# Gathering expert rows on TensorE: one-hot selection for two experts at a time, two down buffers, and norms without GpSimd

## The reference, cut to what matters

```python
x = _ln_affine(ALPHA * x + gate1 * t, ln1_g, ln1_b)      # t: output projection of the mixer
h = (_layer_norm(x) * (1 + scale2) + shift2)             # "h2" in the kernel
f = _hier_moe(h)      # best of 4 groups, best 2 of its 8 experts, for each token
x = _ln_affine(ALPHA * x + gate2 * f, ln2_g, ln2_b)
# an expert: (silu(xb @ w_exp_gate[e]) * (xb @ w_exp_up[e])) @ w_exp_down[e]
```

## Time and profile before

| | us |
|---|---|
| median of 3 runs | 1001.75 (999.08 to 1003.87) |
| the profiled execution: its time | 1002.76 |
| its span, first to last instruction | 1001.2 |
| PE busy | 874.3 (87%) |
| DVE busy | 379.3 (38%) |
| ACT, POOL busy | 209.4, 141.8 |
| HBM read, written | 284.46 MB, 25.45 MB |

### The profile page before, as it was taken

One profiled execution on the slowest core, in us unless ns is written; L12 is line 12 of the kernel. 1 busy time (PEld: TensorE's weight loads), 2 busy tenths in 40 slices (PEclk: granted clock), 3 DMA queues, 4 the chain that ended last, 5 costly groups with the idle time before them and its releaser, 6 DMA issues.

```text
span 1001.2 us, 12712 instructions
## 1 busy us (share of the span) xinstructions
PE 874.3 (87%) x4001; PEld 502.7 (50%) x4002; DVE 379.3 (38%) x672; ACT 209.4 (21%) x302; POOL 141.8 (14%) x192
## 2 busy tenths in 40 slices
PE   3789999999999999969778888997868888887895
PEld 2457677888888887859323233332223233322231
DVE  4522443565343247896412222222122122212145
ACT  2321334441234244122300000000000000000024
POOL 2210267000001000340300000000000000000041
PEclk9799999999999999986999999999999999999998
DMA  9894653365647624449699999999999999999984
GB/s 366 325 299 172 218 206 138 115 236 187 236 181 192 206 86 149 146 158 426 224 419 424 426 426 428 427 426 427 427 428 427 427 427 425 431 425 429 422 337 133
DMA packets 52557, 310.50 MB, mean 310 GB/s; under 512 B 5058, under 2 KB 7202, under 8 KB 36898
## 3 DMA queue, kind: packets, MB, share of 16 engines
q1 hardware_dynamic: 41104, 272.64, 67.2%
q0 software_dynamic: 10800, 35.64, 10.4%
q10 hardware_dynamic: 610, 1.66, 0.6%
HBM read 284.46 MB, written 25.45 MB: 310 GB/s over the span
## 4 chain that ended last, share of the span: by engine, by line
PE 60%; DMA 22%; DVE 6%; issue 3%; SPq 3%; ACT 3%; POOL 1%; DVEq 0%; POOLq 0%; ACTq 0%
PE bank L684 58%; DMA up_w<-in_w_exp_up 18%; DMA modraw<-in_w_mod 2%; SPq L385 2%; PE bank L942 1%; DVE hid L1888 1%; ACT sg L1297 1%; DVE res L1661 1%; DMA y_first<-round_y,pos_y 1%; DMA packed_x<-h,pos 1%; ACT hid_t L1072 1%; PE bank L881 1%; PE bank L876 1%; POOL packed_x L608 1%; DMA round_y<-yout 0%
## 5 line engine op out<-in xcount | busy, mean ns | idle before, releaser
L684 PE MATMUL bank<-gate_w,x_t 128*64 128x512 f32 x512 | 234.2, 611 | 28.7 <-DMA up_w<-in_w_exp_up 20.6
L684 PE MATMUL bank<-up_w,x_t 128*64 128x512 f32 x512 | 234.3, 612 | 0.0
L684 PEld LDWEIGHTS bank<-gate_w,x_t 128*64 128x64 f32 x512 | 70.6, 141 | 183.4 <-issue 180.0
L684 PE MATMUL bank<-down_w,hid_t 128*64 128x512 f32 x496 | 121.7, 636 | 14.7 <-ACT hid_t L1072 14.7
L684 PE MATMUL bank<-h_hi,w_hi 128*128 128x512 f32 x320 | 126.5, 395 | 1.6 <-ACT h_hi L1106 1.6
L684 PE MATMUL bank<-h_hi,w_lo 128*128 128x512 f32 x320 | 126.3, 395 | 0.0
L684 PE MATMUL bank<-h_lo,w_hi 128*128 128x512 f32 x320 | 125.0, 398 | 0.0
L1888 DVE TENSOR_TENSOR hid<-bank,sg 64x512 f32<-64x512 f32 x31 | 21.5, 693 | 226.7 <-ACT sg L1297 226.7
L1437 DVE TENSOR_TENSOR w_lo<-raw,w_hi 128x1024 fp32r<-128x1024 f32 x56 | 68.6, 1227 | 78.6 <-ACT w_hi L1072 78.5
L1297 ACT ACTIVATE sg<-bank 64x512 f32<-64x512 f32 x31 | 18.3, 590 | 378.8 <-PE bank L684 378.8
L615 POOL DMA_DIRECT2D round_y<-yout x31 | 16.1, 519 | 423.3 <-issue 423.3
(11 more groups left out here) (328 smaller groups left out, 1005.8 us busy)
## 6 DMA issues: line engine op xcount, KB each, us to landing
down_w<-in_w_exp_down SPq DMA_DIRECT2D x32, 2048.0 KB, 30.3
gate_w<-in_w_exp_gate SPq DMA_DIRECT2D x31, 2048.0 KB, 24.9
up_w<-in_w_exp_up SPq DMA_DIRECT2D x31, 2048.0 KB, 29.6
modraw<-in_w_mod SPq DMA_DIRECT2D x24, 1024.0 KB, 8.4
raw<-in_w_in SPq DMA_DIRECT2D x9, 2048.0 KB, 9.7
round_y<-zrow POOLq DMA_DIRECT2D x6, 2048.0 KB, 7.6
xrows<-packed_x SPq DMA_DIRECT2D x32, 256.0 KB, 20.9
raw<-in_w_branch_b SPq DMA_DIRECT2D x2, 2048.0 KB, 9.4
```

Of the source, the lines that this page charges most:

```text
L684: return pe.matmul(out, lhsT, rhs, start=start, stop=stop, skip_group_check=True)
```

## The change

- The table `packed_x`, its scatter, and every load of rows go away. h2 is split into two fp32r parts, `h2_hi` (ACT) and `h2_lo` (DVE, h2 less h2_hi), once, behind expert 0. For a pair of experts DVE writes a one-hot matrix `sel` (128 tokens x 4 tiles x 2 experts x 64 slots, fp32r), and PE multiplies it with the two parts: eight matmuls (4 tiles x 2 parts) give 512 of the 1024 columns of both experts' rows. One half is formed in the even expert and the other in the odd one. ACT copies the result to SBUF (`x_rows`), PE transposes it (4), DVE copies it to `x_t`.
- `h2_hi` takes the place of the third down buffer. There are two for down and still three for gate and up; SP issues gate and up of e, then down of e-1, which waits for `down` of e-3.
- The loop goes over six experts (four times), with six written out ahead.
- Norms: DVE adds the residual itself and takes the sum with it; ACT squares with the mean as its bias and sums (`deviation1`, `deviation2`); DVE applies scale and shift; ACT only brings h2 into the order of chunks (`chunk_order`). POOL does none of it. PE transposes tiles 0, 1 and 2 together right behind the projection.
- Routing: positions in `packed_x` and the tables of starts aren't computed any more.

```diff
-        down_w = [at(f"down_w{s}", [128, FC, D], f32, s * SLOT + 32 * K) for s in range(3)]
+        down_w = [at(f"down_w{d}", [128, FC, D], f32, d * SLOT + 32 * K) for d in range(2)]
+        h2_hi = [at(f"h2_hi{i}", [128, KC, 128], f32r, 2 * SLOT + (32 + 4 * i) * K) for i in range(TILES)]
...
+            def next_down(e, d):
+                done = sp.value_load(tab[0:1, 1, bass.ds(e - 1, 1)], min_val=0, max_val=16)
+                sp.wait_ge(m_sem["ym"], e - 1)
...
+            sp.wait_ge(dve_rt, 2)
+            for e in range(3, 6):
+                next_gate_up(e, e % 3)
+                next_down(e - 1, (e - 1) % 2)
+            with sp.Fori(1, 5) as t:
+                for k in range(6):
+                    next_gate_up(6 * t + k, k % 3)
+                    next_down(6 * t + k - 1, (k + 1) % 2)
...
-            for j in range(2):
-                for i in range(TILES):
-                    pool.indirect_dma_start(packed_x[0:ASSIGN, :], bass.IndirectOffsetOnAxis(pos[:, j, i:i + 1], 0),
...
+            def selected(chosen, bank, c):
+
+                for i in range(TILES):
+                    for piece in (h2_hi, h2_lo):
+                        x = mm(bank[:, :], chosen[:, i, :, :].rearrange("p a s -> p (a s)"), piece[i][:, 4 * c:4 * c + 4, :].rearrange("p k n -> p (k n)"),
+                               start=(i == 0 and piece is h2_hi), stop=(i == TILES - 1 and piece is h2_lo))
+                return x
...
+            def first_norm(i):
+                z, row = z_row[i % 2][:, :], res[:, i, :]
                 ch.sync()
...
+                dve.tensor_scalar(fin[:, 2, i:i + 1], fin[:, 0, i:i + 1], fin[:, 1, i:i + 1], -1.0 / D, ALU.add, ALU.mult).then_inc(dve_mean, 1)
```

More of the change, by code:

```diff
@@ L443, in next_expert @@
                 sp.sem_inc(sp_go, 1)
[L444 to L472, removed]
+                load_down(e, d)
+            sp.wait_ge(dve_rt, 2)
[6 more added lines that the diff above has]
+                    next_down(6 * t + k - 1, (k + 1) % 2)
+            next_down(29, 1)
             for e in (30, 31):
-                next_expert(e, e % 3)
-                load_further_rows(e)
+                next_gate_up(e, e % 3)
+                next_down(e, e % 2)
             for i, written, count in ((0, pool_f, 1), (2, f_o, 2), (1, pool_f, 2)):
@@ L656, in expert @@
                     store(yout[s], turn, y_st[s], CAP)
-                further_rounds(e, off, more, first)
+                further_rounds(e, more, first)
             with pool.Fori(0, 10) as t:
@@ L955, in expert @@
                 else:
-                    pe.wait_ge(e_gu[s], 32 * (turn + 1))
-                pe.wait_ge(m_sem["xt"], e + 1)
-                gate_up(x_t[s], s, B[0], m_sem, halves=(e_gu[s], 32 * (turn + 1)) if last else None)
+                    pe.wait_ge(e_gu[s], loaded)
+                pe.wait_ge(m_sem["xt"], e + 1 if opening or second else e - a + 2)
+                gate_up(x_t[:, 2 * a:2 * a + 2, :, :], s, B[0], m_sem, halves=(e_gu[s], loaded) if last else None)
                 if last:
-                    pe.wait_ge(dve_sel, 11)
+                    pe.wait_ge(dve_sel, 6)
                     for i in range(TILES):
@@ L963, in expert @@
                     x.then_inc(pe_sel, 1)
-                def next_rows():
-                    n = (s + 1) % 3
-                    pe.wait_ge(e_x[n], 16 * (turn + 1 + (1 if n == 0 else 0)))
-                    x_transposes(xrows[n], B[2], m_sem)
-                opening = isinstance(e, int) and e == 0
-                if not (last or opening):
-                    next_rows()
+                if opening:
+                    selected_alone(1, B[2]).then_inc(m_sem["xs"], 1)
+                elif second:
+                    pe.wait_ge(dve_h2lo, TILES)
+                    pe.wait_ge(m_sem["sl"], 2)
+                    selected(sel, B[2], 0).then_inc(m_sem["xs"], 1)
+                elif chooses:
+                    pe.wait_ge(m_sem["xt"], e + 2)
+                    if a == 0:
+                        pe.wait_ge(m_sem["sl"], 3 * turn + k // 2 + 2)
+                    selected(sel, B[2], a).then_inc(m_sem["xs"], 1)
@@ L977, in expert @@
+                if opening:
+                    pe.wait_ge(act_rt, 2 * TILES + 1)
+                else:
                     pe.wait_ge(m_sem["yo"], e)
-                down(hid_t_x if opening else hid_t, s, B[1], m_sem)
+                down(hid_t, d, B[1], m_sem)
+                if second:
+                    pe.wait_ge(m_sem["xt"], 3)
+                    selected(sel, B[2], 1).then_inc(m_sem["xs"], 1)
+                    pe.wait_ge(m_sem["xr"], 4)
+                    x_transposes(x_rows, B[2]).then_inc(m_sem["xtr"], 1)
@@ new lines, in chunk_order @@
+            def chunk_order(i):
+                act.wait_ge(dve_h2, i + 1)
+                copy(h2[i][:, :, :], z_row[i % 2][:, :].rearrange("t (p k) -> t k p", k=KC)).then_inc(act_h2, 1)
+            for i in range(TILES - 1):
+                deviation1(i)
+                if i:
+                    chunk_order(i - 1)
+                deviation2(i)
+            deviation1(3)
+            for hb in range(2):
+                h2_columns(0, hb, (B[4], B[5]))
+            for hb in range(2):
+                h2_columns(1, hb, (B[0], B[1]))
@@ L1319, in expert @@
                 opening = isinstance(e, int) and e == 0
-                gate_silu(m_sem, B[0], sg_x if opening else sg, e, 0)
+                second = isinstance(e, int) and e == 1
+                chooses = not (isinstance(e, int) and e >= NEXP - 2)
+                if opening:
+                    act.wait_ge(dve_rt, 2)
+                gate_silu(m_sem, B[0], sg_hid, e, 0)
+                if chooses:
+                    rows_in(e + 2 if opening or second else e + 3)
                 if turns is not None:
@@ new lines, in gated_half, with inverse_root @@
+                dve.wait_ge(dve_gated, h + 1)
+                row = res[:, h // 2, 512 * (h % 2):512 * (h % 2) + 512]
+                ch.did(dve.scalar_tensor_tensor(out=row, in0=part, scalar=1.0, in1=row, op0=ALU.mult, op1=ALU.add,
+                                                accum_out=fin[:, h % 2, h // 2:h // 2 + 1]))
+            def inverse_root(table, i, roots):
+                root, var, inv, tmp = (table[:, k, i:i + 1] for k in (4, 5, 6, 7))
+                dve.wait_ge(act_sq, roots)
+                ch.did(dve.tensor_scalar(var, table[:, 3, i:i + 1], -0.5 / D, -0.5 * EPS, ALU.mult, ALU.add))
+                link(dve.reciprocal(inv, root))
+                link(dve.tensor_scalar(tmp, inv, inv, var, ALU.mult, ALU.mult))
+                link(dve.tensor_scalar(inv, tmp, 1.5, inv, ALU.add, ALU.mult))
@@ L1884, in expert @@
+            def expert(e, k, turn, turns=None):
+                s = k % 3
                 opening = isinstance(e, int) and e == 0
-                last = turns is not None
-                gated_hid, silu = (hid_x, sg_x) if opening else (hid, sg)
+                second = isinstance(e, int) and e == 1
+                chooses = not (isinstance(e, int) and e >= NEXP - 2)
                 dve.wait_ge(m_sem["silu"], e + 1)
-                dve.tensor_tensor(gated_hid[:, :], B[0][CAP:128, :], silu[:, :], ALU.mult).then_inc(m_sem["hid"], 1)
+                dve.tensor_tensor(sg_hid[CAP:128, :], B[0][CAP:128, :], sg_hid[0:CAP, :], ALU.mult).then_inc(m_sem["hid"], 1)
@@ L1915, in _ @@
-            for k in range(3):
+                    dve.tensor_scalar(side[:, 0, 0:3], n0[:, k:k + 3], -0.5, None, ALU.is_gt).then_inc(dve_g, 1)
+                    dve.tensor_scalar(side[:, 1, 0:3], n0[:, k:k + 3], -0.5, None, ALU.is_le).then_inc(dve_g, 1)
+                if not (isinstance(e, int) and e < 3):
+                    dve.wait_ge(y_st[s], 32 * (2 * turn + k // 3))
+                gate_of_slots(yout[s], dve_g, 20 * turn + 2 * (k // 3 + 1) + 2 * k, side[:, 0, s:s + 1], side[:, 1, s:s + 1])
@@ new lines, in expert @@
+                if opening:
+                    for i in range(TILES):
+                        dve.wait_ge(act_h2hi, i + 1)
+                        dve.tensor_tensor(h2_lo[i][:, :, :], h2[i][:, :, :], h2_hi[i][:, :, :].bitcast(f32), ALU.subtract).then_inc(dve_h2lo, 1)
+                dve.wait_ge(m_sem["ym"], e + 1)
+                dve.tensor_tensor(yout[s][:, :], B[1][:, :], yout[s][:, :], ALU.mult).then_inc(m_sem["yo"], 1)
+                if second:
+                    last_chunks(4)
+                    chosen_pair(sel, slot_of[:, 4:6, :]).then_inc(m_sem["sl"], 1)
```

708 lines of the change are left out of this document (299 added, 409 removed).

## The result

| | before | after | forecast |
|---|---|---|---|
| median of 4 runs, us | 1002.79 (999.08 to 1003.87) | 1015.81 (1012.03 to 1020.07) | 980 (964 to 998) |
| span of the profiled execution | 1001.2 | 1013.6 | 980.0 |

The ratio after to before is 1.0138, with a 95% interval of 1.0089 to 1.0187. The forecast was wrong in its sign, and the time lies outside its range.

The account below looks back on a forecast made before the run. Bytes bound the kernel before; after, TensorE was to decide, 14 us later than the bytes. Its path reached expert 30 at 921.9, plus 58.1 gave span 980.0; plus 1.6 less 1.0 gave 980.6, stated as 980 us (964 to 998).

Parts of the forecast that it names:

- expert 0's `gate_up` ends: Start of the experts' stage on TensorE: expert 0's gate matmuls begin at 469.0 and end at 476.1 us.
- to that of expert 2: TensorE through experts 0 and 1, with fp32 selection and a second selection that nothing covers: 34.0 us.
- 28 periods: Experts 2 to 29 on TensorE at 13.8 us each, 386.4 us together.
- further round of expert 19: Expert 19's extra pass: 15.98 us before, now 21.5 with 16 selecting matmuls (3.5) and two copies on the path.
- losses: TensorE's extra time in the experts' stage from first code reads and short clock falls: 11 us, bounds 0 and 25.
- end, from expert 30's `gate_up`: Stretch from expert 30's start to the end: 59.8 less 1.7 for the lower clock before, 58.1 us.
- the prediction's own sign of being wrong: In the experts' stage: an expert of more than 14.3 us, or losses beyond 25.
- The second rival: Loop code on PE is read again in each turn: up to 30 us, taken at half, 995 us; chance 0.15.
- The front: Norms to first loads: h2 8 us sooner (451.4), logits 455.9, gate matmuls 469.0, SP's first waiting load 22 us sooner (476.4).
- The price of the selection: Eight selecting matmuls per expert on TensorE take 1.75 us, like the mixer's form, giving 13.8 us an expert.
- the third rival: TensorE becomes dearer than DMA was: selection near 3.65 us, 15.7 us an expert, end at 1033; chance 0.09.
- The forecast's bound of 966.1: End by the bytes: DMA takes 429.9 us from 476.4 to 906.3, then 59.8 us to the end.

Follow-up runs that it names:

- e1: The kernel after with PE's further-round code left out at five of the loop's six places (same matmuls for this input): 987.69 us, ratio to before 0.984.
- e2: The kernel after with PE's experts 0 to 29 all written out and no loop on PE, nothing left out: 990.30 us, ratio to before 0.988.
- e6: The kernel after without PE's further-round code at the sixth place in the loop (body of 1622 instructions): 987.78 us, ratio to before 0.984.
- e7: The kernel after without PE's further-round code at the fifth and sixth places in the loop (body of 1459 instructions): 987.44 us, ratio to before 0.984.
- e9: e6 with PE's code shifted by 85 semaphore increments at its start: 986.76 us, ratio to before 0.984.
- e10: e6 with PE's code shifted by 170 semaphore increments at its start: 998.74 us, ratio to before 0.995.
- e8: e1 without any further round (expert 19's tokens beyond 64 left out, so the result changes): 971.55 us, ratio to before 0.968.
- e12: e1 with only `h2_hi` in the selection (four selecting matmuls, not eight) and no further round, so the result changes: 970.39 us, ratio to before 0.968.

## Why the prediction was wrong, by its own steps

The path goes over TensorE, so it can be followed by the silus of the experts, which start when `gate_up` ends. Expert 0's is the exception: its `gate_up` ends at 477.8, and silu starts at 479.14, behind a table load of 1.28 us on ACT, which PE doesn't wait for. Expert 2's silu starts at 513.35, expert 30's at 962.20:

| step | forecast | measured | difference |
|---|---|---|---|
| expert 0's `gate_up` ends | 476.1 | 477.8 | +1.7 |
| to that of expert 2 | 34.0 | 35.5 | +1.5 |
| 28 periods | 13.8 each | 13.84 | +1.1 |
| further round of expert 19 | 21.5 | 26.1 | +4.6 |
| losses | 11 (0 to 25) | 35.2 | +24.2 |
| end, from expert 30's `gate_up` | 58.1 | 58.5 | +0.4 |

These make 33.5 of the 33.6 us between 980.0 and 1013.6.

- **The step that failed is the losses.** I put 11 with bounds of 0 and 25. Measured are 35.2: 9.0, 8.0 and 8.6 at the three turns (6.0 to 6.3 us of gap and what the half clock takes), 6.8 in the second gaps of three passes and 2.8 in small ones. Losses beyond 25 were the prediction's own sign of being wrong. I counted first reads as losses of six or twelve experts, and took the loop's fewer turns for a saving; each turn was the dearest place. The runs in which no branch leads back to code that is gone (e1, e2, e6, e7, e9, e10) have no gap behind `down` at the turns.
- **The second rival was the mechanism, and it was priced and weighed too low.** "Up to 30 us, taken at half" was 32.4 (25.6 and 6.8). Its size came from the first passes of before, where a gap is 2.9 us at most; a branch back to code that is gone costs twice that, and the clock falls behind it. And its chance was 0.15, with the count of blocks on the edge in view: "about seven of eight". With the 30 us taken in full it would have given 1010, still below what was measured. The Trainium skill ("Runtime: NRT & Kernel Launch", Instruction fetch mechanics) gives 128 KiB for TensorE, which is 2048 instructions; here 1785 were already too many, nine blocks being read in each pass, and 1622 were not. Its sentence that a taken branch to a page that isn't held must fetch it before execution goes on agrees with the 6.18 us at the turn. But it speaks of a window of two pages, and here bodies of 970 to 1622 instructions (3.8 to 6.3 blocks) run whole passes without a packet, so the measurement decides. Its advice to unroll agrees with e2.
- **The front was right** to 0.4 to 1.7 us, the 8 us on h2 (7.6) and the 22 us on SP's first load (20.6) included. How near it came is in part luck: the projection ended 2.8 us late, and h2 was complete 9.4 us behind its end where I had 11.8. The same front also moves from run to run: expert 0's silu starts at 475.0 to 479.5 in the runs with this front in which the increments don't delay the start.
- **The price of the selection was right.** The period is 13.84 us, 0.04 above the forecast, so the eight selecting matmuls take about what their form in the mixer took, and the third rival (15.7 us an expert) is out.
- **The further round was mis-sized**: 26.1 in place of 21.5. The 16 selecting matmuls take 5.49 us where I had 3.5, partly at half clock (0.60 from 781 to 785 us). DVE forms `sel_x` ahead of them (0.70), 0.56 us of issue stand ahead of ACT's copy, and the 56 instructions behind the round take 14.17 us in place of 12.5; I had none of these three.
- **The bytes.** The forecast's bound of 966.1 leaned on DMA being busy through the further round. It stands for as much as 12.8 us there (e1). Without that round the spans are 969.2 (e8) and 967.1 (e12), so the rest of that bound was right.
- **Without the gaps the sum holds**: e1's span is 985.7 against 980.0. Expert 0's `gate_up` ends 0.6 later, experts 0 and 1 -0.2, periods +1.1, further round +5.5, losses 8.2 in place of 11 (around a wait for down, with some half clock behind), end +1.4.

A version that beats both kernels and leaves nothing out is `e2_unrolled`, 1.2% below before. With a loop's body of at most 1622 instructions the change gives 1.6% (e6, e7; for this input, since they leave out code that it doesn't use).

## What to carry to other kernels

Count the instructions of a loop's body on the engine that will be the bottleneck, and set them against the largest body that is known to stay (here 1622; 1785 didn't), before counting what its instructions do. A change that doubles a body to fit two periods of buffers can lose more there than it gains, and its sign shows as "issue" at the turns of the loop, with instruction packets that come back in each pass. If the body is too long, leave out code or unroll it. And when a change takes the work off the resource that bound the kernel, its losses on the next one are no longer covered: price them in full.

## What the runs showed of the hardware

- A PE loop of 1785 instructions is read again in every pass, nine packets of 16 KB, at three alignments; one of 1622 isn't at three alignments. A turn costs 6.0 to 6.3 us of gap without a shift and 8.4 to 8.9 in two gaps with one of 58 or 140, and without a shift 1.7 to 2.9 us more while the clock is at half.
- Reading forward costs little: 27 packets in 360 us with three gaps of 1.9 to 3.1 us, 2.6 us more than the short loop in the median, with overlapping intervals.
- A semaphore increment on PE takes 153 ns (first matmul at 13.93, 22.34 and 26.93 us behind 85, 140 and 170 of them), so padding of some hundred instructions in front can cost more than what it is to test.
